# Half of the V combination moved from TensorE to VectorE in a PEER layer

## The reference, cut to what matters

```
sc = einsum('chpd,hpnd->chpn', q, sub_keys)
... # top 16 per half, top 16 of the sums: experts, gate g = softmax(best)
u_sel = u[experts]
v_sel = v[experts]
h = gelu(einsum('cd,chkd->chk', xc, u_sel))
act = h * g
return einsum('chk,chkd->cd', act, v_sel)      # and the residual is added
```

## Time and profile before

| | us |
|---|---|
| median of 3 runs (range) | 984.31 (978.98 to 986.7) |
| the profiled execution's own time | 984.35 |
| its span in the trace | 982.6 |
| busy: PE / DVE / ACT / POOL | 648.2 / 502.1 / 228.2 / 542.4 |
| TensorE's mean granted clock, share of full | 0.84 |
| moved by the gathers | 268.47 MB of 297.87 MB |

### The profile page before, as it was taken

One profiled execution on the slowest core, in us unless ns is written; L12 is line 12 of the kernel. 1 busy time (PEld: TensorE's weight loads), 2 busy tenths in 40 slices (PEclk: granted clock), 3 DMA queues, 4 the chain that ended last, 5 costly groups with the idle time before them and its releaser, 6 DMA issues.

```text
span 982.6 us, 6736 instructions
## 1 busy us (share of the span) xinstructions
PE 648.2 (66%) x2005; PEld 357.6 (36%) x2005; DVE 502.1 (51%) x1216; ACT 228.2 (23%) x494; POOL 542.4 (55%) x535
## 2 busy tenths in 40 slices
PE   6999999950049805980498059706960795069998
PEld 5777778840024302430143024302420342034443
DVE  6587537879790299028802990398049204820000
ACT  6687531121002300230023002301220122012221
POOL 6000002785865675567656755675567557765552
PEclk9999999985569956995699569957995898579999
DMA  9734114986898999899989998999899889998886
GB/s 335 253 137 159 44 43 157 361 314 237 315 348 303 330 404 342 303 334 368 340 303 332 410 354 307 338 410 343 308 351 410 324 315 352 368 329 308 303 307 231
DMA packets 91973, 297.87 MB, mean 303 GB/s; under 512 B 8721, under 2 KB 17058, under 8 KB 91938
## 3 DMA queue, kind: packets, MB, share of 16 engines
q0 software_dynamic: 73728, 268.47, 74.6%
q1 hardware_dynamic: 18210, 28.98, 8.7%
HBM read 296.36 MB, written 1.05 MB: 303 GB/s over the span
## 4 chain that ended last, share of the span: by engine, by line
PE 49%; POOL 27%; issue 9%; DVE 7%; DMA 6%; ACT 1%; SPq 0%; POOLq 0%
PE bank L1169 39%; POOL u_rows L360 26%; PE bank L952 5%; DMA v_rows<-in_peer_v_dram,expert 5%; POOL v_rows L369 1%; PE bank L1010 1%; PE bank L1152 1%; DVE w_lo L641 1%; DMA u_rows<-in_peer_u_dram,expert 1%; DVE t_nmax L671 1%; DVE key_idx L828 1%; DVE logits L668 1%; DMA x_sb<-in_x_dram 0%; DVE key_val L825 0%; PE bank L937 0%
## 5 line engine op out<-in xcount | busy, mean ns | idle before, releaser
L1169 PE MATMUL bank<-v_rows,diag 128*128 128x512 f32 x1024 | 454.3, 607 | 314.8 <-DMA v_rows<-in_peer_v_dram,expert 314.8
L1169 PEld LDWEIGHTS bank<-v_rows,diag 128*128 128x128 f32 x1024 | 199.2, 195 | 569.3 <-issue 569.0
L900 DVE CUSTOM_DVE_ANT_0 u_rows<-u_rows,xg 128x1024 f32<-128x1024 f32 x256 | 312.5, 1226 | 88.9 <-DMA u_rows<-in_peer_u_dram,expert 80.0
L369 POOL DMA_INDIRECT v_rows<-in_peer_v_dram,expert x256 | 246.1, 961 | 193.3 <-PE bank L1169 173.0
L360 POOL DMA_INDIRECT u_rows<-in_peer_u_dram,expert x256 | 276.1, 1079 | 111.8 <-issue 77.1
L597 ACT ACTIVATE diag<-ident,act_w 128x128 f32<-128x128 f32 x256 | 101.4, 400 | 610.4 <-PE bank L1169 609.5
L913 DVE TENSOR_TENSOR act_w<-h_gelu,gate 128x32 f32<-128x32 f32 x8 | 1.5, 192 | 255.0 <-ACT h_gelu L590 255.0
L1152 PE MATMUL bank<-featT,w_raw 128*128 128x256 f32 x256 | 58.0, 380 | 0.7 <-ACT featT L563 0.4
L1152 PEld LDWEIGHTS bank<-featT,w_raw 128*128 128x128 f32 x256 | 47.4, 190 | 7.0 <-issue 1.3
L952 PE MATMUL bank<-w_hi,xn_hi 128*128 128x512 f32 x112 | 45.5, 406 | 0.2 <-DVE xn_lo L764 0.2
L952 PE MATMUL bank<-w_hi,xn_lo 128*128 128x512 f32 x112 | 43.8, 391 | 0.0
(11 more groups left out here) (149 smaller groups left out, 408.1 us busy)
## 6 DMA issues: line engine op xcount, KB each, us to landing
w_raw<-in_w_in_dram SPq DMA_DIRECT2D x12, 1024.0 KB, 7.2
w_raw<-in_peer_w_query_dram SPq DMA_DIRECT2D x8, 1024.0 KB, 5.3
w_raw<-in_w_out_dram SPq DMA_DIRECT2D x4, 1024.0 KB, 5.1
u_rows<-in_peer_u_dram,expert POOLq DMA_INDIRECT x256, 6.5
v_rows<-in_peer_v_dram,expert POOLq DMA_INDIRECT x256, 5.4
x_sb<-in_x_dram SPq DMA_DIRECT2D x2, 512.0 KB, 3.8
out_dram<-y_rows SPq DMA_DIRECT2D x2, 512.0 KB, 4.7
g_row<-in_norm_g_dram SPq DMA_DIRECT2D x1, 512.0 KB, 13.1
```

The source lines that it names most:

```text
L369: pool.indirect_dma_start(v_rows[:, n % V_RING, :], None, peer_v[0], bass.IndirectOffsetOnAxis(ap=expert[:, i, h, s:s + 1], axis=0))\
L900: dve.tensor_tensor_reduce(out=u_rows[:, n % U_RING, :], in0=u_rows[:, n % U_RING, :], in1=xg[:, h, :], scale=1.0, scalar=0.0, op0=ALU.mul ...
L1169: ins = mm(ps[4 + 2 * h + c][:, :], diag[:, n % DIAG_RING, :], v_rows[:, n % V_RING, c * COLS:(c + 1) * COLS], start=False, stop=True, ski ...
```

## The change

In the V blocks TensorE keeps half 0: one diagonal per gather of half 0 (128 in all, 256 before), and the two products each. Half 1 goes to VectorE: `combine(i)` runs 16 times, each adding `v_rows * act_w` to the running sum `y_rows[:, 1, :]` by one `scalar_tensor_tensor` of 128x1024 float32, all of its tensors in SBUF. Each of these waits for its gather and for the one before it. VectorE's list becomes dots(i), combine(i - 1), route(i + 2), weights(i), and at the end combine(7). The residual of half 1 is first copied from banks 6 and 7 into `y_rows` by ScalarE (two copies of 128x512). So that the two users take turns, the gathers of a block now alternate between the halves, in U and V blocks alike; `v_used` is one semaphore for each half, and buffer n of the V ring comes free by the user of its own half. The final copy of half 1 falls away; the store of half 1 waits for VectorE's last sum.

```diff
@@ store
-                sp.wait_ge(y_ready[h], 2)
+                if h:
+                    sp.wait_ge(v_used[1], GATHERS // HALVES)
+                else:
+                    sp.wait_ge(y_ready[0], 2)
@@ gather_u, gather_v
-                h, s = divmod(pair, TOPK)
+                s, h = divmod(pair, HALVES)
...
-                need(pool, v_used, n - V_RING + 1)
+                need(pool, v_used[h], (n - V_RING) // HALVES + 1)
@@ diagonal
+                i, s = divmod(m, TOPK)
+                need(act, v_used[0], m - DIAG_RING + 1)
+                act.activation(diag[:, m % DIAG_RING, :], ident[:, :], ACT.Copy, scale=act_w[:, i, 0, s:s + 1])\
+                   .then_inc(diag_ready, 1)
 
+            act.wait_ge(query_done, HP)
+            for c in range(2):
+                act.activation(y_rows[:, 1, c * COLS:(c + 1) * COLS], ps[6 + c][:, :], ACT.Copy).then_inc(y_seeded, 1)
@@ VectorE
+            def combine(i):
+
+                for s in range(TOPK):
+                    m = i * TOPK + s
+                    n = i * PAIRS + HALVES * s + 1
+                    dve.wait_ge(v_landed[n % V_RING], 16 * (n // V_RING + 1))
+                    need(dve, v_used[1], m)
+                    dve.scalar_tensor_tensor(y_rows[:, 1, :], v_rows[:, n % V_RING, :], act_w[:, i, 1, s:s + 1], y_rows[:, 1, :],
+                                             ALU.mult, ALU.add).then_inc(v_used[1], 1)
+
             for i in range(PEER_HEADS):
                 dots(i)
+                if i:
+                    if i == 1:
+                        dve.wait_ge(y_seeded, 2)
+                    combine(i - 1)
                 if i + 2 < PEER_HEADS:
                     route(i + 2)
                 weights(i)
-
-            dve.wait_ge(v_used, GATHERS)
-            dve.tensor_copy(y_rows[:, 1, 0:COLS], ps[6][:, :]).then_inc(y_ready[1], 1)
+            dve.wait_ge(act_ready, PEER_HEADS)
+            combine(PEER_HEADS - 1)
@@ TensorE
-            for n in range(GATHERS):
-                h = n % PAIRS // TOPK
-                pe.wait_ge(diag_ready, n + 1)
+            for m in range(GATHERS // HALVES):
+                n = HALVES * m
+                pe.wait_ge(diag_ready, m + 1)
                 pe.wait_ge(v_landed[n % V_RING], 16 * (n // V_RING + 1))
                 for c in range(2):
-                    ins = mm(ps[4 + 2 * h + c][:, :], diag[:, n % DIAG_RING, :], v_rows[:, n % V_RING, c * COLS:(c + 1) * COLS],
+                    ins = mm(ps[4 + c][:, :], diag[:, m % DIAG_RING, :], v_rows[:, n % V_RING, c * COLS:(c + 1) * COLS],
                              start=False, stop=True, skip_group_check=True)
-                ins.then_inc(v_used, 1)
+                ins.then_inc(v_used[0], 1)
```

More of the change, by code:

```diff
@@ L249, in layer @@
         diag_ready = sem("diag_ready")
-        v_used = sem("v_used")
-        y_ready = [sem(f"y_ready{h}") for h in range(HALVES)]
+        v_used = [sem(f"v_used{h}") for h in range(HALVES)]
+        y_seeded = sem("y_seeded")
+        y_ready = [sem("y_ready0")]
         def need(eng, s, value):
@@ L590, in gelu, with diagonal @@
                 act.activation(h_gelu[:, i, :, :], h_dot[:, i, :, :], ACT.Gelu).then_inc(gelu_done, 1)
[L592 to L597, removed]
+            def diagonal(m):
+                i, s = divmod(m, TOPK)
+                need(act, v_used[0], m - DIAG_RING + 1)
+                act.activation(diag[:, m % DIAG_RING, :], ident[:, :], ACT.Copy, scale=act_w[:, i, 0, s:s + 1])\
                    .then_inc(diag_ready, 1)
+            act.wait_ge(query_done, HP)
+            for c in range(2):
+                act.activation(y_rows[:, 1, c * COLS:(c + 1) * COLS], ps[6 + c][:, :], ACT.Copy).then_inc(y_seeded, 1)
             gate_exp(0)
@@ L606, in _ @@
                 act.wait_ge(act_ready, i + 1)
-                for n in range(i * PAIRS, (i + 1) * PAIRS):
-                    diagonal(n)
-            act.wait_ge(v_used, GATHERS - TOPK)
+                for m in range(i * TOPK, (i + 1) * TOPK):
+                    diagonal(m)
+            act.wait_ge(v_used[0], GATHERS // HALVES)
             for c in range(2):
                 act.activation(y_rows[:, 0, c * COLS:(c + 1) * COLS], ps[4 + c][:, :], ACT.Copy).then_inc(y_ready[0], 1)
-            act.wait_ge(v_used, GATHERS)
-            act.activation(y_rows[:, 1, COLS:D], ps[7][:, :], ACT.Copy).then_inc(y_ready[1], 1)
         @block.vector
@@ L897, in dots @@
                 for n in range(i * PAIRS, (i + 1) * PAIRS):
-                    h, s = divmod(n % PAIRS, TOPK)
+                    s, h = divmod(n % PAIRS, HALVES)
                     dve.wait_ge(u_landed[n % U_RING], 16 * (n // U_RING + 1))
```

## The result

The kernel now takes **1015.22 us** (median of 4 runs, 1010.2 to 1021.28), against 984.98 before (4 runs, 978.98 to 986.7): a ratio of **1.032, interval 1.025 to 1.039**. Ratios, here and in the experiments, are taken from the runs in the faster of a kernel's two states alone, so they need not be the quotient of the medians shown. The direction was forecast (slower had a chance of 0.50) and the time lies in the range, but 30 us were lost where I had 11. The profiled execution has a span of 1010.7, where the sum gave 993.1.

What follows compares the result with a forecast made beforehand. TensorE's products in V blocks and GpSimd's gathers in U blocks bound it. 283.2 unchanged, then five rounds of 103.7 plus 3 for U3 to 804.7, last row landed at 986.3, 6.8 for the end: 993.1, plus 1.75: 995 us; range 955 to 1040.

Steps and rivals of the forecast that it cites:

- What bounds it, and that TensorE goes: V blocks were paced by TensorE's products, 39% of the span; its work per V block halves, to 0.86 us per gather.
- Rival 3, the clock: V blocks: TensorE's clock falls to its low level, giving 1.72 us per gather and 1070 us; chance 0.09.
- The steady pace of 1.28: Steady U blocks: VectorE and GpSimd keep step at 1.28 us per gather, taken as the lower end for V blocks.
- The price of the sum: VectorE in V blocks: one 128x1024 `scalar_tensor_tensor` takes 1.3 us with its wait; sixteen are 21 us.
- The routing behind the combine: VectorE behind a V block's last sum: routing and weights take 12.4 us per round, and GpSimd stops for about 10.
- the hold: GpSimd: a gather that starts inside a VectorE instruction with two SBUF inputs waits until it ends; 0.24 us per gather at random starts.
- the ring: V blocks: gathers paced by the six buffers (landing, products, release); a theory of the experiments, not priced in the forecast.
- Dot products: VectorE in U blocks after a routing: 45.7 us per block, taken from U block 1; bounds 36.6 and 49.
- From the end of dots to the end of the combine: Each of five rounds: -6.3 for V gathers already out, 44.0 of gathers, landing 6.6, last sum 1.3: 45.6 us.
- the pace p: V blocks: time per gather, taken as 1.42 us, between 1.28 and 1.79; 0.01 more adds 2.5 us to the span.
- Rival 1, no holds: V blocks: the sums never hold GpSimd, so 1.28 us per gather and 960 us, down to 936; chance 0.22.
- From the span to the time: Whole kernel: the profiled execution's own time is 1.75 us more than the span of 993.1, giving 995 us.

Runs made afterwards that it cites:

- experiment 9: The kernel before, with the tokens that the dot products read from U block 1 on copied to PSUM: 968.21 us, ratio 0.984.
- experiment 5: The changed kernel, with the routing cut into pieces, three after each of a block's sixteen sums: 959.52 us, ratio 0.968.
- experiment 4: The changed kernel, with one idle TensorE product after each dot product of U1 to U7, to keep the clock high: 1003.99 us, ratio 1.019.
- experiment 1: The changed kernel, with half 1's running sum kept in PSUM, two operations of 512 columns per gather: 1024.2 us, ratio 1.041.
- experiment 2: The changed kernel, with eight V buffers in place of six: 1010.14 us, ratio 1.027.
- experiment 3: The changed kernel, with both sums in PSUM and eight V buffers: 958.42 us, ratio 0.972.
- experiment 10: The changed kernel with routing cut up, sums in PSUM, eight V buffers, and the dot products' tokens in PSUM as well: 915.75 us, ratio 0.931.
- experiment 7: The changed kernel with routing cut up between the sums, sums in PSUM and eight V buffers: 890.1 us, ratio 0.905.

## Why the prediction was right in sign and wrong in size

**What bounds it, and that TensorE goes**: right. The chain changed from products to landings.

**Rival 3, the clock**: excluded as a bound (0.93 to 1.00 in windows of the eight V blocks). But what it does at a block's head was missed, see below.

**The steady pace of 1.28**, the lower end of p: the number was right, but it is the pace of the transfers at 410 GB/s and not of VectorE and GpSimd keeping step (experiment 9).

**The price of the sum** (1.3): measured 1.285.

**The routing behind the combine** (12.4): measured 12.3 in each of the five rounds. Cutting it up between the sums took 56 us off (experiment 5), as much as removing the hold and the ring together (57), so as a whole stop of GpSimd with a slow restart it was half of what the change cost.

**Dot products** (45.7 each): 49.3, 45.6, 47.0, 45.8 and 44.7, a sum of 232.4 against 231.5 with the 3 for U3. The one row on which this rested, U block 1 of the kernel before, was a fair sample, since what made it slow, the held gathers, was confirmed by experiment 9.

**From the end of dots to the end of the combine** (45.6): this is the step that failed. It measured 48.0, 47.8, 47.3, 50.3 and 46.5, in all 12 us more, and the last blocks, which hang on the same pace, 5 us more: nearly all of the 17.6 by which the span is longer. The term is the pace p, 31p in each round. I had built it out of one mechanism, the hold, at 0.18 per gather. In its place the runs showed two: the hold adds 0.13 to the 1.24, and the ring of six buffers the other 0.12 (26 us of waits, all of them for buffers that TensorE frees). Some 16 us of it fall at the heads of the blocks, where the first products run at the low clock; by experiment 4 about half of that is the clock's doing. Behind the head the ring has a limit of its own at about 1.40. I had the buffers in view only as `v_used` of half 1, and never asked how long a cycle of one of TensorE's buffers takes once the products no longer set the pace. The 1.42 that I took was right for the blocks' inner part by accident: the reason given for it would have had the pace fall to 1.24 without holds, and experiment 1 shows that it does not.

**Rival 1, no holds**: wrong for this kernel, and its time, 960, is what the kernel takes when the hold and the ring are both removed (958.4, p of 1.25 to 1.31). Removing the hold alone, which is all that the rival names, did not give it (1024.2, experiment 1).

**From the span to the time**: the profiled execution took 1012.5, 1.8 more than its span, as costed; the median lies 2.7 above it. With the 17.6 these are the 20 us between 995 and 1015.

By the rule of the Trainium skill that the forecast leaned on (GPSIMD Engine Reference, "Key points", contention with VectorE instructions of two SBUF inputs), moving one operand to PSUM had to free GpSimd. The runs agree: 1069 to 968 ns and, in experiment 9, 1.99 to 0.94 us.

## What to carry to other kernels

When the bound is to be removed from a stage, price the next one as if it were alone: for gathers through a ring, (issue to landing + use + release) / buffers, and the first turn of the ring at the clock that the consumer has then. When two limits are of about the same size, an experiment that removes one shows little or nothing in the time; remove both before a theory is given up. Work that ran free beside the old bound, here 12 us of routing, is better put between the new instructions than behind them: that was worth 56 us.

## What the runs showed of the hardware that I had not expected

- A gather on GpSimd that starts inside a VectorE instruction with two float32 inputs in SBUF does not proceed until that one ends: 1.99 us against 0.94. With one of the two in PSUM it is not held (0.94). That held for the dot products (16 us of the kernel before by the medians, experiment 9) and for the sums (52 us with eight buffers, 1010.1 to 958.4, experiments 2 and 3).
- The hold was smaller than starts at random would make it, 0.13 per gather and not 0.24.
- A sum of 1024 columns in SBUF took 1285 ns; in PSUM it took two instructions of 752 ns by the group, and 1.41 us for the pair in the timeline.
- The gathers' transfers reached 410 GB/s in U blocks, one gather of 512 KB per 1.28 us, at a DMA share of 1.03. In no trace did a stretch of 20 us in the PEER part move more than 412. GpSimd can issue them a little faster for a block (1.26 in V block 1 of experiment 3), and there they took longer to land, 7.3 us at the median against 6.1.
- VectorE's chains of short instructions had gaps of up to about 1.2 us, some longer, in some kernels (experiments 1, 2, 9 and 10) and none in others (the changed kernel and experiment 3). In experiment 1 they went on when GpSimd had stopped. In experiment 10, slower in all than experiment 7, they stand where the gathers ran free throughout. Their cause is not known.
